# Gated-delta stage of a two-block kernel: head lengths from two-part squares, one convolution tap on ScalarE, modulation sums and three panels placed elsewhere, output banks held longer

## The reference

```python
mod = (silu(c) @ w_ada + b_ada)          # 6 x 1024: shift1, scale1, gate1, shift2, scale2, gate2
h = rms_norm(x, norm1_w) * (1 + scale1) + shift1
proj = h @ w_in                          # gq, gk, gv, gz, ga, gb, sq, sk, sv
qkv = silu(causal_depthwise_conv(concat(gq, gk, gv), conv_w))   # 4 taps, 1536 channels
q_g, k_g = l2_norm(heads(gq)), l2_norm(heads(gk))               # 8 heads of 64 each
o_g = gated_delta_rule_chunked(q_g, k_g, v_g, g, beta)          # 8 chunks of 64 tokens
o_s = sliding_window_attention(...)
x = x + gate1 * (concat(o_g, o_s) @ w_out)
x = x + gate2 * ffn(rms_norm(x, norm2_w) * (1 + scale2) + shift2)
```

## Time and profile before

| what | us |
|---|---|
| median of 3 runs | 1245.25 (1245.01 to 1246.96) |
| profiled execution, its time | 1245.2 |
| profiled execution, its span | 1243.4 |
| TensorE busy in the span | 1218.1 |
| VectorE busy | 708.4 |
| ScalarE busy | 492.7 |

### The profile page before, as it was taken

One profiled execution on the slowest core, in us unless ns is written; L12 is line 12 of the kernel. 1 busy time (PEld: TensorE's weight loads), 2 busy tenths in 40 slices (PEclk: granted clock), 3 DMA queues, 4 the chain that ended last, 5 costly groups with the idle time before them and its releaser, 6 DMA issues.

```text
span 1243.4 us, 19952 instructions
## 1 busy us (share of the span) xinstructions
PE 1218.1 (98%) x8398; PEld 994.4 (80%) x8398; DVE 708.4 (57%) x1040; ACT 492.7 (40%) x774; POOL 107.5 (9%) x152
## 2 busy tenths in 40 slices
PE   6999999999999999999999999999999999999998
PEld 4777878878888888888888889898876778888886
DVE  6699978655476553333333567768665554333344
ACT  4343643664346222212222343215475662322232
POOL 4000005511030000000000110000012310000000
PEclk9999999999999999999999999999999999999999
DMA  9557711003033542243322342333123025333311
GB/s 342 211 189 222 237 35 37 3 4 104 2 101 103 169 158 78 79 127 102 102 77 64 98 136 78 102 93 83 49 69 81 1 73 140 89 90 106 106 34 68
DMA packets 149928, 125.58 MB, mean 101 GB/s; under 512 B 15952, under 2 KB 133489, under 8 KB 149712
## 3 DMA queue, kind: packets, MB, share of 16 engines
q1 hardware_dynamic: 148416, 121.98, 32.3%
q0 software_dynamic: 1232, 2.07, 0.6%
q10 hardware_dynamic: 192, 0.27, 0.1%
HBM read 122.20 MB, written 2.10 MB: 100 GB/s over the span
## 4 chain that ended last, share of the span: by engine, by line
PE 86%; DVE 9%; ACT 2%; issue 2%; DMA 1%; DVEq 0%; POOL 0%; ACTq 0%
PE bank L611 50%; PE bank L913 6%; PE bank L718 4%; PE bank L1386 4%; PE bank L1356 4%; PE bank L1420 4%; DVE post L2212 2%; DVE arena L2331 2%; PE bank L1275 2%; DVE wlo L2180 1%; PE bank L749 1%; PE bank L1102 1%; PE bank L669 1%; PE bank L1311 1%; PE bank L1328 1%
## 5 line engine op out<-in xcount | busy, mean ns | idle before, releaser
L611 PE MATMUL bank<-hsplit,whi 128*128 128x512 f32 (+1 forms) x1840 | 541.4, 378 | 1.9 <-DVE wlo L2180 1.9
L611 PEld LDWEIGHTS bank<-hsplit,whi 128*128 128x128 f32 x1840 | 334.9, 188 | 73.4 <-issue 9.5
L611 PE MATMUL bank<-hsplit,wlo 128*128 128x512 f32 (+1 forms) x920 | 346.1, 376 | 0.0
L2180 DVE TENSOR_TENSOR wlo<-ring,whi 128x2048 fp32r<-128x2048 f32 (+4 forms) x100 | 200.4, 2005 | 175.1 <-ACT whi L1625 174.8
L1625 ACT ACTIVATE whi<-ring 128x2048 fp32r<-128x2048 f32 (+4 forms) x100 | 168.6, 1686 | 122.8 <-DVE xT L2579 53.3
L611 PEld LDWEIGHTS bank<-hsplit,wlo 128*128 128x128 f32 x920 | 172.9, 188 | 32.3
L611 PE MATMUL bank<-a_split,whi 128*128 128x512 f32 x340 | 104.7, 389 | 0.0
L611 PEld LDWEIGHTS bank<-a_split,whi 128*128 128x128 f32 x340 | 63.8, 188 | 13.3
L611 PE MATMUL bank<-a_split,wlo 128*128 128x512 f32 x170 | 66.1, 389 | 0.0
L1568 POOL TENSOR_TENSOR acc<-acc,tb 128x512 f32<-128x512 f32 x12 | 17.7, 1478 | 424.5 <-ACT tb L1883 424.5
L1629 ACT ACTIVATE a_split<-tb 128x512 fp32r<-128x512 f32 x22 | 13.8, 632 | 88.1 <-DVE tb L2629 87.9
(11 more groups left out here) (488 smaller groups left out, 1793.8 us busy)
## 6 DMA issues: line engine op xcount, KB each, us to landing
ring<-in_w_in_dram SPq DMA_DIRECT2D x22, 1024.0 KB, 5.3
ring<-in_w_in_dram SPq DMA_DIRECT2D x34, 512.0 KB, 5.2
ring<-in_w_ada_dram SPq DMA_DIRECT2D x16, 1024.0 KB, 5.1
ring<-in_w_gate_dram SPq DMA_DIRECT2D x11, 1024.0 KB, 5.3
ring<-in_w_up_dram SPq DMA_DIRECT2D x11, 1024.0 KB, 5.4
ring<-in_w_down_dram SPq DMA_DIRECT2D x8, 768.0 KB, 4.7
ring<-in_w_down_dram SPq DMA_DIRECT2D x8, 640.0 KB, 4.2
hscratch<-in_w_ada_dram SPq DMA_DIRECT2D x4, 1024.0 KB, 14.7
```

What stands on the lines that cost most here:

```text
L611: last = mm(o[0:m, 0:n], w[:, k, c0:c0 + m], rhs(s, k), start=k + i == 0, stop=k == kn - 1 and i == 2)
L2180: split_lo = splitter(dve, None, lambda lo, src, hi: tt(lo, src, hi, ALU.subtract))
```

## The change

1. Head lengths: ScalarE copies each square into an fp32r high part (`hsq_split`), VectorE makes the rest (`length_lo`), and TensorE sums both with two fp32r matmuls in place of one float32 matmul. `pick` is copied to fp32r once. Lengths of tile m are now summed after the projection of tile m+5 and not m+4.
2. Convolution: the tap of the current token is applied by ScalarE, in a second read of the bank (`conv_in` is two instructions); VectorE does three taps and no TENSOR_SCALAR.
3. Modulation sums: part 4 in VectorE's prologue, in two halves; 5 and 6 after tiles 5 and 9 (before: 4, 5, 6, 7 after tiles 3, 5, 7, 9); 7 where 8 was, 8 where 9 was, and 9 after the last split. TensorE's `ada(i)` and the panels in the ring move with them.
4. Third panel: `qkv2` is split ahead of the first tile's copy and convolution on both engines.
5. `go` banks: each is let go two chunks later than before.
6. The loads: `ada40` and `ada41` stand ahead of `qkv3`, the constants behind them.

```diff
+        hsq_split = arena_r[:, 12 * T:18 * T].rearrange("p (s b t) -> p s b t", s=2, b=3)
+        pick_r = arena_r[:, 18 * T:18 * T + CONST_W["pick"][1]]
...
         for i in range(6):
             cols_panel(f"qkv{i}", w_in, 256 * i)
-            if i in (3, 4, 5):
-                ada_panel(1 + i)
+            if i in (2, 4):
+                ada_panel(4 + (i - 2) // 2)
         panel("abk", KD, 168, [(0, 32, w_cols(w_in, 2048, 32)), (32, 8, w_cols(w_in, 2056, 8)),
                                (40, 128, w_cols(w_in, 2576, 128))])
+        ada_panel(6)
+        cols_panel("sv", w_in, 2704, 128)
         ada_panel(7)
-        cols_panel("sv", w_in, 2704, 128)
+        for i in range(2):
+            cols_panel(f"sq{i}", w_in, 2064 + 256 * i)
         ada_panel(8)
         for i in range(2):
-            cols_panel(f"sq{i}", w_in, 2064 + 256 * i)
+            cols_panel(f"gz{i}", w_in, 1536 + 256 * i)
         ada_panel(9)
-        for i in range(2):
-            cols_panel(f"gz{i}", w_in, 1536 + 256 * i)
...
-        SPLIT_AT = (0, 2, 5, 7, 9, 11)
+        SPLIT_AT = (2, 5, 7, 9, 11)
...
             def head_lengths(m):
 
                 if m == 0:
                     length_tile[0] = open_tile(pe, "hsum", hold=True)
-                    pe.wait_ge(*arrived("const_rest"))
-                pe.wait_ge(*done("hsq", m))
-                last = mm(length_tile[0][0:40, :], pick[:, m // 4, m % 4, :], hsq[m % 2], start=m == 0, stop=m == 7)
+                    pe.wait_ge(*done("act_vectors", "pick"))
+                pe.wait_ge(*done("dve_vectors", "hsq_lo", m))
+                for s in range(2):
+                    last = mm(length_tile[0][0:40, :], pick[:, m // 4, m % 4, :], hsq_split[:, s, m % 3, :],
+                              start=m + s == 0, stop=m + s == 8)
...
-                if m >= 4:
-                    head_lengths(m - 4)
-                if m >= 7 and m % 2 == 1:
-                    ada((m - 7) // 2 + 4)
+                if m >= 5:
+                    head_lengths(m - 5)
+                if m in (7, 11):
+                    ada(4 + (m - 7) // 4)
             project(("ab",), "abk", 0, P, hx, T)
+            head_lengths(7)
...
-            amid_sq = [{1: [(ada, 7)]}, {3: [(query_lengths, 0)]}, {3: [(query_lengths, 1)]}, {1: [(query_lengths, 2)], 4: [(ada, 8)]}]
-            amid_gz = [{1: [(ada, 9)], 3: [(query_lengths, 3)], 5: [(gate_cols,)], 7: [(gate_rows, 0)]},
-                       {3: [(gate_rows, 1)]}, {1: [(gate_rows, 2)], 7: [(gate_rows, 3)]}, {}]
+            amid_sq = [{1: [(ada, 6)]}, {3: [(query_lengths, 0)]}, {3: [(query_lengths, 1)]}, {1: [(query_lengths, 2)], 4: [(ada, 7)]}]
+            amid_gz = [{1: [(ada, 8)], 3: [(query_lengths, 3)], 5: [(gate_cols,)], 7: [(gate_rows, 0)]},
+                       {3: [(gate_rows, 1)]}, {1: [(gate_rows, 2)], 7: [(gate_rows, 3)]}, {5: [(ada, 9)]}]
...
                     if n % 2:
                         last.then_inc(*fill("go", n // 2))
-                        let_go("go", n // 2)
+                        if n > 1:
+                            let_go("go", n // 2 - 1)
...
+            let_go("go", NB - 1)
...
-                if name == "ada40":
+                if name == "qkv3":
                     sp.dma_start(consts[:, CONST_FIRST:], a["consts"][:, CONST_FIRST:]).then_inc(sem("ld_const_rest"), 16)
...
             def conv_in(m):
                 act.wait_ge(*filled("pj", m))
                 if m >= 3:
-                    act.wait_ge(*done("conv", m - 3, 3))
-                A(raw[m % 3][:, 3:], bank("pj", m)[:, :], ACT.Copy).then_inc(*read("pj", m))
+                    act.wait_ge(*done("conv", m - 3, 2))
+                A(raw[m % 3][:, 3:], bank("pj", m)[:, :], ACT.Copy)
+                A(qkv[:, m, :], bank("pj", m)[:, :], ACT.Copy, scale=V2[:, 36 + m:37 + m]).then_inc(*read("pj", m))
...
             def head_square(m):
                 if m >= 2:
-                    act.wait_ge(*done("hsum_step", m - 2))
+                    act.wait_ge(*done("dve_vectors", "hsq_lo", m - 2))
                 act.wait_ge(*done("silu", m))
                 A(hsq[m % 2], qkv[:, m, :], ACT.Square).then_inc(*signal("hsq", m))
-
+                if m >= 3:
+                    act.wait_ge(*done("hsum_step", m - 3))
+                act.wait_ge(*done("hsq", m))
+                A(hsq_split[:, 0, m % 3, :], hsq[m % 2], ACT.Copy).then_inc(*signal("act_vectors", "hsq_hi", m))
+
+            split_hi()
...
             scale_half(1)
+            ada_sum(4, 0)
             ada_mod(1)
...
-                ts(qkv[:, m, :], raw[m % 3][:, 0:T], tap(0), None, ALU.mult).then_inc(*signal("conv", m, 0))
-                for k in range(1, 4):
-                    dve.wait_ge(*done("conv", m, k - 1))
+                for k in range(3):
+                    if k:
+                        dve.wait_ge(*done("conv", m, k - 1))
                     stt(out=qkv[:, m, :], in0=raw[m % 3][:, k:k + T], scalar=tap(k), in1=qkv[:, m, :],
                         op0=ALU.mult, op1=ALU.add).then_inc(*signal("conv", m, k))
 
+            ada_sum(4, 1)
+            split_lo()
+            def length_lo(m):
+
+                if m >= 3:
+                    dve.wait_ge(*done("hsum_step", m - 3))
+                dve.wait_ge(*done("act_vectors", "hsq_hi", m))
+                tt(hsq_split[:, 1, m % 3, :], hsq[m % 2], hsq_split[:, 0, m % 3, :].bitcast(F32), ALU.subtract)\
+                    .then_inc(*signal("dve_vectors", "hsq_lo", m))
+
             for m in range(12):
                 conv4(m)
+                if m >= 4:
+                    length_lo(m - 4)
                 if m == 1:
                     meta_scaled()
                 if m in SPLIT_AT:
                     split_lo()
-                if m % 2 and m >= 7:
-                    ada_mod(4 + (m - 7) // 2)
-                if m in (3, 5, 7, 9):
-                    ada_sum(4 + (m - 3) // 2)
-            ada_sum(8)
+                if m in (7, 11):
+                    ada_mod(4 + (m - 7) // 4)
+                if m in (5, 9):
+                    ada_sum(5 + (m - 5) // 4)
+            ada_sum(7)
             split_lo()
...
-            ada_mod(7)
-            ada_sum(9)
+            ada_mod(6)
+            ada_sum(8)
...
+            ada_mod(7)
             ada_mod(8)
-            ada_mod(9)
-            dve.wait_ge(*copied("ada", 9))
-            stt(out=modA2, in0=modT[:, 32:40], scalar=1.0, in1=col("norm2", 0, 8), op0=ALU.add, op1=ALU.mult)\
-                .then_inc(*signal("dve_vectors", "modA2"))
+            ada_sum(9)
+
+            def second_scale():
...
                 decay_mul(j)
+            second_scale()
```

More of the change, by code:

```diff
@@ L727, in h_ready @@
                 return lambda k: done("h" + tag, k)
-            pick = cst("pick").rearrange("p (w j c) -> p w j c", w=2, j=NJ)
+            pick = pick_r.rearrange("p (w j c) -> p w j c", w=2, j=NJ)
             length_tile = [None]
@@ L1676, in conv_in @@
                 if m >= 3:
-                    act.wait_ge(*done("conv", m - 3, 3))
-                A(raw[m % 3][:, 3:], bank("pj", m)[:, :], ACT.Copy).then_inc(*read("pj", m))
+                    act.wait_ge(*done("conv", m - 3, 2))
+                A(raw[m % 3][:, 3:], bank("pj", m)[:, :], ACT.Copy)
+                A(qkv[:, m, :], bank("pj", m)[:, :], ACT.Copy, scale=V2[:, 36 + m:37 + m]).then_inc(*read("pj", m))
             def conv_out(m):
-                act.wait_ge(*done("conv", m, 3))
+                act.wait_ge(*done("conv", m, 2))
                 A(qkv[:, m, :], qkv[:, m, :], ACT.Silu).then_inc(*signal("silu", m))
@@ L1700, in _ @@
                     conv_out(m - 2)
+                if m == 3:
+                    act.wait_ge(*arrived("const_rest"))
+                    A(pick_r, cst("pick"), ACT.Copy).then_inc(*signal("act_vectors", "pick"))
                 if 3 <= m < 11:
                     head_square(m - 3)
-            act.wait_ge(*arrived("const_rest"))
             for r0 in (0, HD):
@@ L2193, in spread, with ada_sum @@
                     last.then_inc(*(signal("diag" + tag) if b == 3 else signal("part")))
-            def ada_sum(i):
+            def ada_sum(i, half=None):
                 if i in (3, 1):
@@ L2202, in ada_sum @@
                 halves = 1 if i < 4 else 2
-                for h in range(halves):
+                for h in range(halves) if half is None else (half,):
                     h = 1 if i == 3 else h
+                    if h and halves == 2:
+                        dve.wait_ge(*done("adapart", i))
                     dve.wait_ge(*ada_loaded(i, h))
@@ L2215, in ada_sum @@
                     last.then_inc(*signal("adaacc" if h == halves - 1 or i == 3 else "adapart", i))
-                    if h < halves - 1:
-                        dve.wait_ge(*done("adapart", i))
             def ada_mod(i):
@@ L2393, in _ @@
             split_lo()
+            ada_mod(7)
             ada_mod(8)
-            ada_mod(9)
-            dve.wait_ge(*copied("ada", 9))
```

(8 more changed lines are left out.)

## The result

The changed kernel takes **1248.17 us** (median of 12 runs, 1245.71 to 1250.02), the kernel before 1245.43 beside it (12 runs, 1245.01 to 1247.3). The ratio is 1.0018, with a 95% interval of [1.001, 1.0025]: 2.7 us slower. Forecast were 1244.8 and a range up to 1247.5. The profiled execution took 1247.83 us, with a span of 1245.8. Of the 12 runs, two took 1245.71 and 1245.97 us, at a mean granted clock of 0.998 and 0.997; the other ten, 1246.87 and more, had 0.995 or 0.996. All but those two and the one of 1246.87 lie above the range.

What follows compares the result with a forecast made beforehand. TensorE bounds the kernel, with VectorE also full in the qkv stage. Terms: -0.2 at abk, +0.92 for the moved ada, -1.2 for the banks, about 0.0 elsewhere: -0.4 on 1245.2 gives 1244.8 us; range 1241.5 to 1247.5.

Steps and rivals of the forecast that it cites:

- TensorE's prices: In the qkv stage: a tile costs 5.55 us, a length's matmul pair 0.50, together 6.05; 8 lengths save 4.8.
- That two matmuls cost as much as one: Rival at the head lengths: the fp32r pair costs 0.98 us like the float32 matmul, giving 1246.7; within the forecast's 0.64.
- The prologue: VectorE's first half of sum 4 starts at 45.2, takes 2.9 us and fits inside its idle wait by 0.9.
- The wait at length 0: TensorE, there at 73.6, waits 2.2 us for VectorE's subtraction, done at 75.7.
- The chain behind it: After length 0, TensorE waits for VectorE's subtraction 1.7 us at length 2 and 2.4 at length 6.
- the three waits: TensorE's waits for VectorE at lengths 0, 2 and 6, 6.3 us together, use up what TensorE saves.
- `abk` starts at 112.3 + 6.3 = 118.6: TensorE reaches abk at 112.3 without waits, plus 6.3 us of waits, against 118.76 before.
- The banks and sum 9: Held go banks remove TensorE's 1.2 us wait in the recurrence; sum 9 behind the last split costs nothing, at most 1.5.
- The ring: Rival: loads issued together share DMA engines, qkv3 lands at 71.0, length 0 is 4.8 us later, 1249.6; within slower's 0.14.
- that rival decides: The ring rival in the qkv stage decides when the qkv3 load lands after 66.2.
- the forecast's own sign of being wrong: No TensorE wait at length 0 or 6, or ScalarE waiting for qkv3 beyond 66.
- TensorE's saving comes through: Rival: subtractions in time, abk starts at 112.3, 1238.9 at best; decides at 2.2 us more VectorE lead; chance 0.22.

Runs made afterwards that it cites:

- e1: The changed kernel with each head length summed one tile later on TensorE (length m after tile m+6): 1237.02 us, ratio 0.9932.
- e11: The changed kernel with 10 useless 512-column matmuls on TensorE ahead of its wait at length 6 alone: 1246.89 us, ratio 1.0006.
- e4: The kernel before with only the go banks held as in the change: 1243.82 us, ratio 0.9986.
- e6: The changed kernel with the current tap back on VectorE (four taps, one bank read by ScalarE), lag of five: 1250.74 us, ratio 1.0041.
- e7: e1 with the current tap back on VectorE: 1238.98 us, ratio 0.9948.
- e9: e1 with VectorE repeating the subtraction for length 6 eight times before the one that signals: 1239.97 us, ratio 0.995.
- e8: e1 with the modulation sums, their panels and the third panel's split where they were before: 1242.70 us, ratio 0.9979.
- e5: The changed kernel with VectorE subtracting for length m-4 ahead of tile m's taps, not behind them: 1240.43 us, ratio 0.996.
- e10: e1 with VectorE repeating the subtraction for length 6 ten times: 1241.90 us, ratio 0.9965.
- e2: The changed kernel with 14, 6 and 10 useless 512-column matmuls on TensorE ahead of lengths 0, 2 and 6: 1246.79 us, ratio 1.0011.
- e12: e10 with 11 useless 512-column matmuls on TensorE ahead of length 6: 1242.74 us, ratio 0.9973.

## Why the prediction was wrong

- **TensorE's prices** held within 0.14. A tile and a pair were to be 6.05 (0.50 for the pair); in e1 they are 5.91 (97.69 to 103.60), the pair alone, from 84.91 to 85.37, is 0.46, and e1 reaches `abk` at 110.8. That TensorE worked "without a gap" before is not quite so: it waited 0.34 us for a square at its first length, at 68.59. *That two matmuls cost as much as one* falls.
- **The prologue** held: sum 4's first half began at 45.04 (45.2 forecast), and neither half costs time that shows.
- **The wait at length 0 was mis-sized**: 2.2 forecast, 3.49 measured. The sum 11.25 + 1.2 + 2.2 + 0.68 for VectorE had no ScalarE in it. It takes qkv2's rest as done at 60.35 (60.86 measured, 0.3 of it from a later start of the whole) and leaves out the 0.27 and 0.80 for ScalarE's reads. ScalarE's order was read only up to 58.1. The next panel in it is `qkv3`, which the new order of the loads brings late, so it stands 2.27 us in front of `qkv3`, with tile 3 behind it.
- **The chain behind it** held to 0.2 us: from length 0 to length 2 I had 13.8 us and it is 13.70; the wait at length 6, 2.4 forecast, is 2.60. At length 2 TensorE waited only 0.19 of the 1.7, because it came 1.5 us late itself, by the clock. That the three waits make 6.3 us, as forecast, is chance: 1.3 too much at length 0 and 0.2 at length 6 against 1.5 too little at length 2.
- **The step that failed** is "`abk` starts at 112.3 + 6.3 = 118.6": a wait taken at its own length, with nothing for what TensorE does slowly behind it. `abk` started at 120.99. Behind length 6 TensorE worked for 6.5 us at a granted clock of 0.50, which cost 3.0 us (e11's 136.97 against 139.96) with no wait behind it to hide them. My length 6 was at 118.6 - 0.92 - 0.50 = 117.2 and came at 118.55, 1.4 late by VectorE; with the clock this makes 4.4, and `gz0` came 4.1 later than my 164.3. The two of the 12 runs with the least loss of clock took 1245.7 and 1246.0 us.
- **The banks and sum 9** held: forecast -1.2, and e4's recurrence is 1.45 shorter, its median 1.7 less. The changed kernel's recurrence is 1.0 shorter still, with fewer gaps called issue. So 4.1 late and 1.3 gained on the forecast's -1.2 make 2.8 of span; the rest up to 3.4 lies outside the span (2.0 us, 1.8 before) and between the profiled execution and the median.
- **The ring** as a shared transfer falls: `qkv3` landed 5.2 us after its issue and `qkv4` behind it, 7.8 after. But the point from which that rival decides, a landing after 66.2, was just reached: ScalarE's split began at 66.29, which is also the forecast's own sign of being wrong (beyond 66). It led to the 1.07 us above, by way of the second reads (e6), and not to 4.8.
- ***TensorE's saving comes through*** was priced at 1238.9 at best and given to a VectorE 2.2 us further ahead. This kernel was one edit away: with one tile more of lag it is 1237.02.

## What to carry to other kernels

When a producer's result is moved behind other work in its queue, count its lead in tiles and give the consumer one more, before pricing the waits: here one tile of lag was worth 11 us, where the cheaper lengths take 8 x 0.52 = 4.2 us off TensorE. Price a longer wait of a dense TensorE by more than its length: ask what it will then do slowly, and whether another engine is late next and hides that. When work is put earlier on one engine, follow the queue of every engine that takes part in it up to the place in question, not just to the end of the moved step.

## What the runs showed of the hardware

- **Clock.** Waits of 1.40 (e7), 1.53 (e9) and 1.74 us (e8) in a stretch where TensorE otherwise had no gap left the granted clock at 1.00. Behind 1.98 (e5), 2.60, 2.98 (e10), 3.07 and 4.86 (e6), 3.40 (e11) and 3.49 us it fell to 0.50, during the wait or up to 2 us after TensorE had started again, and was back at 1.00 3 to 7 us later, TensorE being busy without a gap. The price was 1.5 (behind 3.49), 3.0 (behind 2.60), 1.55 (behind 2.98), 1.57 (behind 1.98) and 2.5 us (behind e11's 3.40), so it does not follow from the wait's length alone. It is a little under half of the time that TensorE worked at the lower level: 3.2, 6.5, 3.4, 3.4 and 5.4 us. Each is from one profiled execution. In the profiled runs this is only 0.2 to 0.6% off the mean clock (0.994 to 0.998), easy to overlook.
- **Issue gaps.** In the three kernels with ten to 30 more TensorE instructions at 74 to 120 us, the recurrence, more than 70 us behind them and the same code, was 1.4 to 2.1 us longer (124.1 to 124.2 us in e2, e11, e12) than in the kernels that they were made from. That the added instructions are the cause is not shown: with none added the profiled executions spread from 122.1 to 123.3 (e6), so about half of this also comes without them. It is as large as many an effect looked for here: with added work as a probe the stage must be read by its rows, not by the total.
